# Shift and scale of the second norm as row sums on VectorE, and an earlier split of the second unit's weights

## What is computed

```
c_act = silu(c)
mod = c_act @ ada_w + ada_b                       # c: 1024, ada_w: 1024 x 6144
sh1, sc1, gt1, sh2, sc2, gt2 = split(mod, 6)
h = rms_norm(x, norm1_g) * (1 + sc1) + sh1
proj = h @ w_in                                   # q, k, v, g, gk, z, xbc (4096), dt, gates
o_a = gla_mixer(...);  o_b = ssd_mixer(...)       # xbc first goes through a causal conv of 4 taps
merged = gate_a * (o_a @ w_oa) + gate_b * (o_b @ w_ob)
x = x + gt1 * (merged @ w_out)
h = rms_norm(x, norm2_g) * (1 + sc2) + sh2
x = x + gt2 * moe(h)                              # 32 experts, top 1 of 4 groups, top 2 of 8 in it
out = rms_norm(x, final_norm_g)
```

## Time and profile before

| | |
|---|---|
| median of 3 runs | 705.91 us (705.42 to 707.85) |
| the profiled execution | 706.34 us, span 704.5 us, mean clock 0.992 |
| TensorE busy | 675.9 us (96%), 5658 matmuls |
| VectorE busy | 402.9 us (57%) |
| ScalarE busy | 264.3 us (38%) |
| GpSimd busy | 70.9 us (10%) |
| moved by DMA | 200.74 MB, mean 285 GB/s |
| chain that ended last | TensorE 81%, VectorE 7%, DMA 5%, ScalarE 3% |

### The profile page before, as it was taken

One profiled execution on the slowest core, in us unless ns is written; L12 is line 12 of the kernel. 1 busy time (PEld: TensorE's weight loads), 2 busy tenths in 40 slices (PEclk: granted clock), 3 DMA queues, 4 the chain that ended last, 5 costly groups with the idle time before them and its releaser, 6 DMA issues.

```text
span 704.5 us, 13267 instructions
## 1 busy us (share of the span) xinstructions
PE 675.9 (96%) x5658; PEld 544.0 (77%) x5658; DVE 402.9 (57%) x685; ACT 264.3 (38%) x372; POOL 70.9 (10%) x69
## 2 busy tenths in 40 slices
PE   8998999999999999999999999999999999999893
PEld 8997999899778777899989998766666666665441
DVE  4656677859977598987856467454323222221226
ACT  3346344535867422535453333332131221211003
POOL 0001000000000624400000000001112111111111
PEclk9999999999999999999999999999999999999997
DMA  9988576876534333336568658989999999999992
GB/s 366 420 343 272 210 292 245 292 259 235 200 126 144 120 120 125 122 118 238 179 239 312 237 184 325 374 297 389 418 382 419 421 420 421 419 419 419 420 360 98
DMA packets 31053, 200.74 MB, mean 285 GB/s; under 512 B 5031, under 2 KB 5415, under 8 KB 7826
## 3 DMA queue, kind: packets, MB, share of 16 engines
q1 hardware_dynamic: 27378, 193.27, 71.2%
q0 software_dynamic: 3616, 6.62, 2.5%
HBM read 194.83 MB, written 10.75 MB: 292 GB/s over the span
## 4 chain that ended last, share of the span: by engine, by line
PE 81%; DVE 7%; DMA 5%; ACT 3%; issue 2%; SPq 1%; POOL 0%; DVEq 0%; ACTq 0%; POOLq 0%
PE ps L1529 79%; DMA ring<-in_expert_pieces 4%; DVE ring_rounded L910 2%; ACT ring_rounded L623 1%; SPq L454 1%; DMA ring<-in_pieces 1%; PE ps L1650 1%; PE ps L1946 1%; DVE r_lm L1023 1%; ACT sq L739 1%; DVE g_sb L1118 0%; DVE r_kq L1149 0%; DVE r_xs_rounded L1205 0%; DVE newton L896 0%; DVE newton L895 0%
## 5 line engine op out<-in xcount | busy, mean ns | idle before, releaser
L910 DVE TENSOR_TENSOR ring_rounded<-ring,ring_rounded 128x2048 fp32r<-128x2048 f32 x60 | 136.9, 2290 | 54.3 <-ACT ring_rounded L623 54.0
L1529 PE MATMUL ps<-hT_rounded,ring_rounded 128*128 128x256 f32 x832 | 150.4, 287 | 4.7 <-DVE ring_rounded L910 3.4
L1529 PEld LDWEIGHTS ps<-hT_rounded,ring_rounded 128*128 128x128 f32 x832 | 129.2, 193 | 8.8 <-issue 7.7
L623 ACT CAST ring_rounded<-ring 128x2048 fp32r<-128x2048 f32 x60 | 114.1, 1904 | 42.2 <-PE ps L1529 27.9
L1529 PE MATMUL ps<-ring_rounded,hT_rounded 128*128 128x512 f32 x352 | 109.7, 393 | 0.9 <-DVE ring_rounded L910 0.9
L1529 PE MATMUL ps<-x_sb_rounded,ring_rounded 128*128 128x256 f32 x416 | 109.8, 284 | 0.0
L1529 PEld LDWEIGHTS ps<-x_sb_rounded,ring_rounded 128*128 128x128 f32 x416 | 77.2, 193 | 0.9 <-issue 0.2
L1529 PEld LDWEIGHTS ps<-ring_rounded,hT_rounded 128*128 128x128 f32 x352 | 64.2, 188 | 15.0 <-DVE ring_rounded L910 1.7
L582 POOL DMA_INDIRECT y_rows<-r_st,r_btm x29 | 28.5, 983 | 347.3 <-DVE r_st L1412 340.7
L834 ACT ACTIVATE sq<-ps 128x128 f32<-128x128 f32 x32 | 8.9, 278 | 141.3 <-PE ps L1529 141.3
L1529 PE MATMUL ps<-ring,r_lm 128*64 128x256 f32 x512 | 59.2, 380 | 1.0 <-DMA ring<-in_expert_pieces 1.0
(11 more groups left out here) (328 smaller groups left out, 996.8 us busy)
## 6 DMA issues: line engine op xcount, KB each, us to landing
ring<-in_pieces SPq DMA_DIRECT2D x74, 1024.0 KB, 5.0
ring<-in_expert_pieces SPq DMA_DIRECT2D x48, 1024.0 KB, 15.6
r_z<-in_expert_pieces SPq DMA_DIRECT2D x12, 1024.0 KB, 12.3
r_xs<-in_expert_pieces SPq DMA_DIRECT2D x12, 1024.0 KB
g_sb<-in_expert_pieces SPq DMA_DIRECT2D x6, 1024.0 KB, 12.6
r_st<-in_expert_pieces SPq DMA_DIRECT2D x6, 1024.0 KB, 13.8
r_bt<-in_expert_pieces SPq DMA_DIRECT2D x6, 1024.0 KB, 18.4
hT<-in_expert_pieces SPq DMA_DIRECT2D x6, 1024.0 KB, 17.8
```

The costliest lines, as they stand in the source:

```text
L623: nc.scalar.copy(high_of(p_), slot_of(p_)).then_inc(hi_ok, 1)
L910: nc.vector.tensor_tensor(low_of(p_), slot_of(p_), high_of(p_).bitcast(F32), ALU.subtract).then_inc(lo_ok, 1)
L1529: return nc.tensor.matmul(o, l, r, start=start, stop=stop)
```

## The change

Blocks ("ada", 6) to ("ada", 9) leave the plan, the ring and both engines. In their place the sixteen vectors of 128 values are computed as row sums. The host lays out `ada_w` transposed, so that a channel is a partition and the 1024 inputs lie along the row: eight new pieces ("row", i, h), two for each i of 6 to 9. `rows_out(i)` on VectorE multiplies the two pieces, each 128 x 2 x 1024, by silu(c), which stands in every partition, and sums each row with `accum_out` into a column of `mod`: four instructions a call. Call 6 stands behind obT, 7 behind oa(1), 8 behind ob(0), 9 behind ob(1) and the next split. The additions of ada_b and norm2 follow. Silu(c) is broadcast by a DMA of GpSimd into r_pv behind the product gtb(0,1) and activated by ScalarE behind gate(3).

The rows go through r_ct and r_v, so each pair waits until the one before has been read, and gate rows 0 and 1, which lay there, are now loaded behind the last call. On SyncE, `load_rows(6)` stands where these gate rows were loaded, `load_rows(7)` behind obT ahead of expert pieces 0 and 1, `load_rows(8)` and `load_rows(9)` where the second pieces of ob(0,0) and ob(1,0) have been used.

Apart from this, ScalarE and VectorE split eight pieces, not seven, ahead of the exponentials of the small projection.

```diff
-ADA_AFTER = {("xbc", i): 3 + i for i in range(1, 7)}
+ADA_AFTER = {("xbc", i): 3 + i for i in range(1, 3)}
...
+ROW_PIECES = [("row", i, h, 0) for i in range(6, 10) for h in range(2)]
+ROWS_AT = {("oa", 1, 1): 7, ("ob", 0, 1): 8, ("ob", 1, 1): 9}
...
+            def load_rows(i):
+                if i > 6:
+                    sp.wait_ge(start_row_read, 4 + 2 * (i - 6))
+                for h in range(2):
+                    sp.dma_start(slot_of(("row", i, h, 0)), piece_src(("row", i, h, 0))).then_inc(s_gate, 16)
+
...
                     mix_wait(sp, ("diag", 3, 1))
-                    for p_q in GATE_ROWS[:2]:
-                        sp.dma_start(slot_of(p_q), piece_src(p_q)).then_inc(s_gate, 16)
+                    load_rows(6)
                 if n >= LOADS and PIECES[n - LOADS] == ("oa", 1, 0, 0):
                     mix_wait(sp, ("obT", 7))
+                    load_rows(7)
                     load_moe(0)
                     load_moe(1)
...
+                if n >= LOADS and PIECES[n - LOADS] in (("ob", 0, 0, 1), ("ob", 1, 0, 1)):
+                    piece_used(sp, PIECES[n - LOADS])
+                    load_rows(8 + PIECES[n - LOADS][1])
...
             load_moe(5)
+            sp.wait_ge(start_row_read, 4 + len(ROW_PIECES))
+            for p_ in GATE_ROWS[:2]:
+                sp.dma_start(slot_of(p_), piece_src(p_)).then_inc(s_gate, 16)
...
+            mix_wait(pool, ("gtb", 0, 1))
+            pool.dma_start(c_rows, c_row.partition_broadcast(P)).then_inc(s_crow_fng, 16)
...
-                    before("small")
+                    split_to(len(START) + 2)
                     nc.scalar.activation(rows[:, 1, :], rows[:, 1, :], ACT.Exp).then_inc(a_exp, 1)
...
+                if i == 3:
+                    act.wait_ge(s_crow_fng, 16)
+                    nc.scalar.activation(c_rows, c_rows, ACT.Silu).then_inc(x_sqrt_crow, 1)
...
-                before("small")
+                split_to(len(START) + 2)
                 bank = mix_wait(dve, "small")
...
-            link(nc.vector.scalar_tensor_tensor(mod[:, 32:40], mod[:, 32:40], 1.0, col("norm2", 0, 8), ALU.add, ALU.mult))
+            def rows_out(i):
+
+                dve.wait_ge(x_sqrt_crow, 2)
+                dve.wait_ge(s_gate, 32 * (i - 5))
+                for h in range(2):
+                    rows_ = slot_of(("row", i, h, 0)).rearrange("p a b -> p (a b)").rearrange("p (m k) -> p m k", m=2)
+                    for m in range(2):
+                        at = 4 * i + 2 * h + m
+                        ins = nc.vector.scalar_tensor_tensor(rows_[:, m], rows_[:, m], 1.0, c_rows, ALU.mult, ALU.mult,
+                                                             accum_out=mod[:, at:at + 1])
+                    ins.then_inc(start_row_read, 1)
...
+            rows_out(6)
...
+                        if (name, i, h) in ROWS_AT:
+                            if (name, i) == ("ob", 1):
+                                before((("out", 0), 0))
+                            rows_out(ROWS_AT[name, i, h])
+            dve.wait_ge(start_row_read, 4 + len(ROW_PIECES))
+            link(nc.vector.tensor_tensor(mod[:, 24:40], mod[:, 24:40], col("ada_b", 24, 16), ALU.add))
+            link(nc.vector.scalar_tensor_tensor(mod[:, 32:40], mod[:, 32:40], 1.0, col("norm2", 0, 8), ALU.add, ALU.mult))
```

More of the change, by code:

```diff
@@ L58 @@
 NCOL = PAR["ident"][0]
-ADA_AFTER = {("xbc", i): 3 + i for i in range(1, 7)}
+ADA_AFTER = {("xbc", i): 3 + i for i in range(1, 3)}
 QUARTERS = KD // 2
-ADA_ORDER = [("quarter", q) for q in range(QUARTERS)] + [("ada", i) for i in range(4, 10)]
+ADA_ORDER = [("quarter", q) for q in range(QUARTERS)] + [("ada", i) for i in range(4, 6)]
 START = [("pair", 0, 0, 0), ("rest", 0, 0, 0), ("pair", 1, 0, 0), ("pair", 2, 0, 0), ("rest", 1, 0, 0), ("pair", 3, 0, 0)]
@@ L139, with trunk @@
     AHEAD_OF[_n] = AHEAD_IN_CONV if _at <= 16 else AHEAD
-def trunk(nc, x, final_norm_g, x_t, params, pieces, small_w, gk2_rows, router_w, gate_bias, expert_pieces, out):
+def trunk(nc, x, final_norm_g, x_t, params, pieces, small_w, gk2_rows, router_w, gate_bias, c_row, expert_pieces, out):
     with ExitStack() as ctx:
@@ L307, in trunk @@
         h2_hi, h2_lo, sel_even, sel_taken2 = (sem(n) for n in "h2_hi h2_lo sel_even sel_taken2".split())
-        start_read, mod_ok, x_sqrt = (sem(n) for n in "start_read mod_ok x_sqrt".split())
+        start_row_read, mod_ok, x_sqrt_crow = (sem(n) for n in "start_then_row_read mod_ok x_sqrt_then_c_rows".split())
         moe_full = [sem(f"moe_full{i}") for i in range(MOE_SLOTS - len(EARLY))] + [
@@ L327, in trunk @@
         fin_sqrt, fin_scaled, out_ready = (sem(n) for n in "fin_sqrt fin_scaled out_ready".split())
-        s_xT, s_x, s_small, s_par, s_const, s_ones, s_wr, s_fng, s_gate = (sem(n) for n in "s_xT s_x s_small s_par s_const s_ones s_wr s_fng s_gate".split())
+        s_xT, s_x, s_small, s_par, s_const, s_ones, s_wr, s_crow_fng, s_gate = (sem(n) for n in "s_xT s_x s_small s_par s_const s_ones s_wr s_crow_fng s_gate".split())
         s_pool = sem("s_pool_chain")
@@ L406, in slot_of @@
                 return gate_at[GATE_ROWS.index(p_)]
+            if p_ in ROW_PIECES:
+                return gate_at[p_[2]]
             return early_at[EARLY.index(p_)] if p_ in EARLY else ring[:, slot_at(PIECE_AT[p_])]
@@ L418, in loaded @@
             elif p_ in GATE_ROWS[:2]:
-                eng.wait_ge(s_gate, 32)
+                eng.wait_ge(s_gate, 16 * len(ROW_PIECES) + 32)
             else:
@@ L442, in piece_src @@
         def piece_src(p_):
+            if p_ in ROW_PIECES:
+                return pieces[len(EARLY) + len(PIECES) + ROW_PIECES.index(p_)]
             return pieces[EARLY.index(p_) if p_ in EARLY else len(EARLY) + PIECE_AT[p_]]
@@ L2064, in packed @@
     of = {"ada": inputs["ada_w"][0], "quarter": inputs["ada_w"][0], "gt": inputs["ada_w"][0], "oa": inputs["w_oa"][0], "ob": inputs["w_ob"][0], "out": inputs["w_out"][0]}
-    pieces = np.empty((len(EARLY) + len(PIECES), P, KD, HC), np.float32)
-    for n, (kind, i, h, r) in enumerate(EARLY + PIECES):
+    pieces = np.empty((len(EARLY) + len(PIECES) + len(ROW_PIECES), P, KD, HC), np.float32)
+    for n, (kind, i, h, r) in enumerate(EARLY + PIECES + ROW_PIECES):
         w, at = (of[kind], 0) if kind in of else (w_in, OFF.get(kind, 0))
@@ L2072, in packed @@
             pieces[n] = by_partition(w_in[i * D // 2:(i + 1) * D // 2, OFF["q"]:OFF["q"] + CW]).reshape(P, KD, HC)
+        elif kind == "row":
+            at = i * CW + h * HC
+            pieces[n] = by_partition(inputs["ada_w"][0][:, at:at + HC].T).reshape(P, KD, HC)
         elif kind == "gt":
@@ L2115, in packed @@
             "router_w": np.concatenate([by_partition(router).reshape(P, -1), router_b], axis=1),
-            "gate_bias": inputs["ada_b"][0][10 * CW:12 * CW].reshape(2, CW), "expert_pieces": experts}
+            "gate_bias": inputs["ada_b"][0][10 * CW:12 * CW].reshape(2, CW), "c_row": inputs["c"][0], "expert_pieces": experts}
 def kernel(**inputs):
```

21 lines of the change are left out of this document (11 added, 10 removed).

## The result

| | before | after |
|---|---|---|
| median | 705.81 us (705.02 to 707.85, 5 runs) | 698.67 us (698.45 to 701.13, 5 runs) |
| profiled execution | 706.34 us, span 704.5 us | 700.86 us, span 699.0 us, mean clock 0.991 |
| TensorE busy | 675.9 us, 5658 matmuls | 669.4 us, 5402 matmuls |
| VectorE busy | 402.9 us | 420.1 us |

Ratio 0.9907 [0.989, 0.9925].

The account below looks back on a forecast made before the run. TensorE was taken to bound the kernel up to the experts, the weight queue the expert stage. 706.34 - 4.9 - 8.1 + 1.5 + 3.8 = 698.6 us profiled, 698.2 median; range 695.5 to 701.5 (chance 0.54).

Parts of the forecast that it names:

- Start, -4.9: Second unit's split ahead of the exponentials removes TensorE's 3.36 us wait and the 1.72 us half-clock loss; bounds 0 and -5.1.
- Four blocks, -8.1: adaLN blocks 6 to 9 off TensorE: 1.88 us each plus one 0.63 us wait; bounds -8.1 and -4.1.
- Row operation, 1.30 us: VectorE's row sums with accum_out: sixteen operations at 1.30 us from start to start, 5.2 us a call.
- Rival 3: Slower: the accumulator halves VectorE's rate, an operation takes 2.45 us, a call 9.8; 714.3 us; chance with neighbours over 708: 0.12.
- rows_out(6), no stall: On VectorE behind obT: pushes later work by 5.2 us, yet subtractions for ob(0,0) arrive in time, 0.3 us of room.
- The stall ahead of the second half of ob(0,1), 1.5: Ring piece ob(0,1,1), fifth behind the wait in SyncE's queue, lands late and stalls TensorE 1.5 us (0 to 2.5).
- Transposes of x2, 2.9 us: rows_out(9) delays out(0)'s evictions, TensorE waits 2.9 us at its transposes; inside the queue's delay, so not added.
- Queue restart, +3.8: Expert-weight queue runs dry near 435, restarts at 440.0 after rows_out(9); end 3.8 us later; bounds 0 to 8.4.
- the first paragraph's: Expert stage: it ends a fixed time after its queue of weights has become busy for good.
- Rival 1: Better: extra transfers hide in the 466 to 472 gap and piece ob(0,1,1) lands in time; 692.9 us; chance 0.09.

Follow-up runs that it names:

- e11: Changed kernel with rows(7) loads behind ring piece ob(0,1,1), rows(7) sums behind the subtraction for ob(0,0), rows(9) sums ahead of ob(1,1)'s eviction: 694.85 us.
- e2: Changed kernel with the early split taken back (seven pieces ahead of the exponentials), blocks still replaced by row sums: 704.82 us, ratio 0.9989.
- e1: Kernel before with the early split alone, eight pieces ahead of the exponentials and the four blocks kept: 700.99 us, ratio 0.9918.
- e4: Changed kernel with gate rows 0 and 1 and their wait moved behind gate rows 2 and 3 and two expert pieces: 698.72 us, ratio 0.9891.
- e8: Changed kernel without the two loads of gate rows 0 and 1, so the second gate is partly computed from wrong weights: 700.57 us, ratio 0.9919.
- e3: Changed kernel with SyncE's load of rows(7) moved behind expert pieces 0 and 1 and ring piece ob(0,1,1): 697.11 us, ratio 0.9859.
- e13: e11 with the rows(9) sums halved: two operations ahead of ob(1,1)'s eviction, two behind the subtraction for out(0): 696.71 us, ratio 0.9863.
- e5: Changed kernel with the edits of e3 and e4 together: 697.5 us, ratio 0.9883.
- e7: Changed kernel without the eight row-piece transfers; the sums stay but go to scratch, second norm's shift and scale zero: 696.73 us, ratio 0.9857.
- e9: Kernel before without blocks 6 to 9 and nothing in their place, second norm's shift and scale zero: 695.99 us, ratio 0.9857.
- e10: Changed kernel with the four sums of rows(9) on VectorE moved ahead of the eviction of ob(1,1): 699.6 us, ratio 0.9915.
- e12: e9 with the early split of e1 added, so blocks left out and no row sums: 692.28 us, ratio 0.9801.

## Why the prediction held, point by point

The time was right (698.2 against 698.67), and in part by luck: the gain and the loss were both too small by about the same amount, and one of its mechanisms isn't there.

- **Start, -4.9.** The wait of 3.36 us and the half clock behind it are gone. In the profiled execution TensorE reaches the transposes behind xbc(1) at 74.51, 3.7 us earlier than before (70.74 + 7.48); in e11's it is 72.60, 5.6 us earlier. The two differ by a stretch at half clock at 62 to 64 us, which some executions have and others don't; e2 has it too, and there it costs nothing, since the old wait behind it absorbs it. The medians say -5.0 (e1), the ratio -5.8. Right, but for the half clock, which in some executions doesn't go but moves to 62 us.
- **Four blocks, -8.1.** Up to A the changed kernel is 13.12 us ahead (369.49 - 356.37); less 3.72 of the start that is 9.4. The step that failed is the price of a block: 4 x 2.03 = 8.1 instead of 7.5, read from a whole unit instead of from two starts; with the wait of 0.63 us, 8.7. Of the last 0.7 us, 0.3 lie in the stretch with the fourth block (36.12 us before for 258 matmuls, 33.76 after for 194) and 0.2 behind it; why isn't shown.
- **Row operation, 1.30 us.** 1.14 from start to start, a call 4.6 instead of 5.2. Rival 3, by which the accumulator would halve the rate, is refuted: the form with accum_out takes 1.22 us, the one without took 1.28. The rule of the Trainium skill that halves the throughput of this instruction with two SBUF sources that are not bf16 (Vector Engine (DVE) Microarchitecture Reference, section 7, Points that are easy to get wrong), as the prediction read it, doesn't agree with these rows, and the measurement decides.
- **rows_out(6), no stall.** Right: TensorE's first new wait is the one of 3.2 us.
- **The stall ahead of the second half of ob(0,1), 1.5.** Right place, mis-sized: 3.2 us of waiting, and 1.7 us of clock behind it that the sum didn't have. The step that failed is the count of what stands in front of the piece: I had it fifth, behind 4 MB; SyncE issued two ring pieces behind the wait, so it was sixth, and landed 14.5 us after its issue, at 381.44 instead of the 379.6 (392.7 less 13.1) I had.
- **Transposes of x2, 2.9 us, "lies inside that and isn't added".** The size was right (2.4), the conclusion wrong: it moves B, and so it is in the time.
- **Queue restart, +3.8.** It restarted at 431.35 (predicted 440.0 less 13 = 427.0, and later than that by the stall and by the waits behind it) and the old gap at 466 to 472 closed as said, but the end didn't follow it (e4, e8): 0 in place of 3.8. The step that failed is the first paragraph's, that the stage ends a fixed time after its queue has become busy for good. The end stands a fixed time behind B, and with it behind the first buffer that TensorE frees, 25.4 us later; the restart's delay was lost in the gap, the term's own lower bound. In the window of 472 to 644 us TensorE, busy for 170.68 of 172 us, waited for no piece; only behind it did the queue make it wait, for the same few pieces before and after.

In the profiled executions: 706.34 - 3.7 - 9.4 + 7.8 (3.2 + 1.7 + 2.4 + 0.5 of gaps too short to place) = 701.0, against 700.86 measured. The prediction had -13.0 + 5.3 = -7.7; this execution has -13.1 + 7.8 = -5.3, and without the half clock at 62 to 64 us it would have some 1.9 us more of gain, 699.0. Loss too small by 2.5, gain too small by 2.0 of what the kernel gives when that stretch is absent: they nearly cancel, and the match within 0.5 us says nothing for the terms.

Rival 1's first half (the extra transfers are hidden in the old gap) is what happened; its second (the piece in time) isn't, and the wait at the transposes took the place of both.

## What to carry to other kernels

A queue at full rate and an engine that is 99% busy beside it can't be told apart by rates. Take two transfers out of the queue: if the same time comes back as idle time of the queue, its bytes up to there are not what sets the end. Then look where the engine's waits for the queue stand; here all of them stood in the last experts. When a wait is put into a DMA queue, count every transfer behind it up to the one that somebody needs, and put that one ahead of the wait; this alone gave 1.6 us of median (698.67 to 697.11), and with two moves on VectorE 3.8. Work moved to an engine with 40% idle time isn't free: what counts is the spare time of the one chain that passes through it, and splitting the work in two within the same chain gains nothing.

## What the runs showed of the hardware

TensorE's clock falls to 0.50 behind some waits and not behind others of the same length. Behind 2.4 us at the transposes of x2 it stayed at 1.00 in the executions of after, e2, e3, e4, e8 and e13, and fell in those of e5 and e7. Behind 3.2 to 3.4 us it fell each time (before, after, e2, e4, e8, e9, e10), behind 1.7 (e3, e5) it didn't; behind 1.9 us it fell in e10 and in the start of e2, behind 2.0 in e11 it didn't. A fall costs 1.5 to 3.4 us on top. And a stretch at 0.50 came without any wait, at 62 to 64 us, in the profiled executions of after, e1, e2, e3, e4, e12 and e13 and not in those of before, e5, e7, e8, e9, e10 and e11. What TensorE did before it is the same in all of them: the 32 matmuls of the small projection, with 48 columns each, which count as busy. The fall at 444.7 us in e7 came behind matmuls of 36 columns. After:

```profile
57.76 3.67 PE L1571 MATMUL ps<-r_z 128*128 128x48 f32 x32
```

Windows behind it (five engines, clock, DMA share, GB/s):

```profile
60.00:62.00 2.00, 2.00 (x17) 2.00 (x17) 2.00 (x7) 1.97 (x3) 0.39 (x1) 0.84 0.97 328
62.00:64.00 2.00, 2.00 (x11) 2.00 (x11) 1.99 (x6) 2.00 (x2) 0.00 (x0) 0.50 0.83 293
64.00:66.00 2.00, 2.00 (x16) 2.00 (x15) 1.93 (x1) 1.55 (x3) 0.00 (x0) 0.81 1.03 420
```

By these rows it costs 0.32 + 1.00 + 0.38 = 1.7 us, against a spread of 2.7 us between a kernel's runs (698.45 to 701.13 for the changed one); the runs without a profile don't show whether it makes that spread. What sets it off in one execution and not in another stays open.
